# mLSTM output products by pairs of heads, sample transposes between the prompt chunks, and the sample state update beside the first attention scores

## What is computed

```python
s = jnp.einsum('blhd,bshd->bhls', q, k) * w_intra
num = (jnp.einsum('bhls,bshv->blhv', s, v)
       + jnp.einsum('bhvd,blhd->blhv', C, q) * jnp.moveaxis(w_inter, 1, 2)[..., None])
den = jnp.sum(s, axis=-1) + w_inter * jnp.einsum('bhd,blhd->bhl', n, q)
den = jnp.maximum(jnp.abs(den), jnp.exp(-m_t))
h = num / jnp.moveaxis(den, 1, 2)[..., None]
C_new = w_state[..., None, None] * C + jnp.einsum('bhs,bshv,bshd->bhvd', w_rows, v, k)
n_new = w_state[..., None] * n + jnp.einsum('bhs,bshd->bhd', w_rows, k)
```

## Time and profile before

| what | us |
|---|---|
| median of 3 runs | 1441.0 |
| lowest and highest of them | 1438.35 and 1442.01 |
| the profiled execution | 1432.52 |
| its span | 1430.7 |
| TensorE busy in the span | 1317.1 (92%) |
| from the first mLSTM score to the first attention score | 722.47 to 789.40 |

### The profile page before, as it was taken

The page is one execution under the profiler, slowest core; times in us unless marked ns, Lnnn a source line. Parts: engine busy times, 40 slices in busy tenths (PEclk is TensorE's granted clock), DMA queues, the critical chain, the costliest instruction groups (busy, mean ns, idle before and its releaser), DMA issues.

```text
span 1430.7 us, 23707 instructions
## 1 busy us (share of the span) xinstructions
PE 1317.1 (92%) x8072; PEld 1147.1 (80%) x8072; DVE 828.3 (58%) x1445; ACT 573.1 (40%) x1131; POOL 319.4 (22%) x276
## 2 busy tenths in 40 slices
PE   4999999999999969999997688969999999999996
PEld 2889999999778858888875355858899999988885
DVE  2666767776435455513335875338777777754545
ACT  4533434433334355322112465336444444433433
POOL 0443343433100000000100604004444444510000
PEclk9999999999999989999975698989999999999998
DMA  9545454544433322221220523112223322212232
GB/s 316 166 148 154 153 159 143 153 147 132 163 109 96 132 63 91 88 88 59 104 60 0 156 75 123 31 73 60 74 73 88 88 87 73 74 59 74 95 132 111
DMA packets 167003, 152.71 MB, mean 107 GB/s; under 512 B 10361, under 2 KB 139777, under 8 KB 166954
## 3 DMA queue, kind: packets, MB, share of 16 engines
q1 hardware_dynamic: 165610, 148.24, 33.0%
q0 software_dynamic: 1344, 3.81, 1.0%
HBM read 142.72 MB, written 9.05 MB: 106 GB/s over the span
## 4 chain that ended last, share of the span: by engine, by line
PE 79%; DVE 10%; issue 4%; ACT 4%; DMA 2%; DVEq 0%; POOL 0%; SPq 0%; ACTq 0%; POOLq 0%
PE ps L1079 76%; DVE resid L1942 1%; DVE w_sums_lo L1723 1%; DVE h_sums_lo L1723 1%; DVE max_den L2217 1%; DMA resid<-in_x_sample 1%; DMA w_raw<-in_w_ffn_in 1%; DVE act_t L1834 1%; DVE silu_gate L1827 1%; DVE w_lo L1723 1%; DVE probs L2226 1%; ACT x_norm L661 1%; PE ps L1121 0%; DVE y L1905 0%; ACT modulated_pairs L712 0%
## 5 line engine op out<-in xcount | busy, mean ns | idle before, releaser
L1079 PE MATMUL ps<-h_sums_hi,w_sums_hi 128*128 128x320 f32 x1216 | 378.0, 315 | 15.3 <-ACT silu_gate L731 5.0
L1079 PE MATMUL ps<-h_sums_hi,w_sums_lo 128*128 128x320 f32 x1216 | 370.7, 309 | 0.0
L1079 PE MATMUL ps<-h_sums_lo,w_sums_hi 128*128 128x320 f32 x1216 | 370.5, 309 | 0.0
L1079 PEld LDWEIGHTS ps<-h_sums_hi,w_sums_hi 128*128 128x128 f32 x1216 | 227.2, 188 | 31.9 <-issue 20.7
L1723 DVE TENSOR_TENSOR w_lo<-w_raw,w_hi 128x512 fp32r<-128x512 f32 (+3 forms) x106 | 99.0, 934 | 230.7 <-ACT w_hi L805 156.1
L1079 PEld LDWEIGHTS ps<-h_sums_lo,w_sums_hi 128*128 128x128 f32 x1216 | 227.2, 188 | 0.0
L1079 PEld LDWEIGHTS ps<-h_sums_hi,w_sums_lo 128*128 128x128 f32 x1216 | 227.1, 188 | 0.0
L1079 PE MATMUL ps<-w_hi,act_hi 128*128 128x512 f32 x440 | 174.0, 395 | 3.6 <-issue 3.6
L1079 PE MATMUL ps<-w_hi,act_lo 128*128 128x512 f32 x440 | 172.1, 391 | 0.0
L1079 PE MATMUL ps<-w_lo,act_hi 128*128 128x512 f32 x440 | 172.1, 391 | 0.0
L1723 DVE TENSOR_TENSOR w_sums_lo<-w_raw,w_sums_hi 128x512 fp32r<-128x512 f32 x136 | 129.1, 955 | 54.8 <-ACT w_sums_hi L749 45.0
(11 more groups left out here) (325 smaller groups left out, 1902.0 us busy)
## 6 DMA issues: line engine op xcount, KB each, us to landing
w_raw<-in_w_ffn_in SPq DMA_DIRECT2D x88, 512.0 KB, 3.8
w_raw<-in_w_ada SPq DMA_DIRECT2D x28, 1024.0 KB, 5.1
w_raw<-in_w_ffn_out SPq DMA_DIRECT2D x88, 256.0 KB, 2.6
w_raw<-in_w_in SPq DMA_DIRECT2D x10, 1024.0 KB, 5.1
w_raw_start<-in_w_ada SPq DMA_DIRECT2D x8, 1024.0 KB, 8.1
w_raw<-in_w_out SPq DMA_DIRECT2D x4, 1024.0 KB, 5.1
k_cache<-in_cache_k SPq DMA_DIRECT2D x8, 512.0 KB, 4.5
v_cache<-in_cache_v SPq DMA_DIRECT2D x8, 512.0 KB, 3.7
```

Of the source, the lines that this page charges most:

```text
L1079: return pe.matmul(out, lhsT, rhs, start=start, stop=stop)
```

## The change

Five things change.

1. PE's output products of a chunk go by pairs: `ST` for heads 0 and 1, then `QST` for heads 0 and 1, then the same for 2 and 3. DVE's `m_hn` waits become one wait for both banks.
2. The sample work is spread over the chunks. DVE writes `QB` for head 0 ahead of chunk 0 and for heads 1, 2 and 3 during chunks 0 and 1; PE transposes one set ahead of and one behind each chunk's output products (queries in chunks 0 and 1, states in chunks 2 and 3), all in bank 7; ACT copies each set between two exponentials. `QBT` has four buffers.
3. In the sample tile the `NROW` transpose and the `WB` products stand together in bank 7, and the 20 output products follow without transposes between them. DVE adds to `NNAT`, spreads the keys of heads 0 and 1 and scales `SC` while they run.
4. The prompt's final transposes and copy (to a tile of its own, `FIN`) come right behind these products, then the new states of heads 0 and 1, then the scores of attention steps 0 and 1, and then the new states of heads 2 and 3. DVE takes the first maxima and then adds all four new states and spreads the last two heads' keys.
5. The waits that stood ahead of the first score move to the first attention transposes and outputs. SP's `GH` loads wait for `st_tr` 5, and POOL's transfers out of `SC` for all of the new state.

```diff
-        QB = at("q_by_batch", N0, [P, DB, DQ]); N0 += 2 * KB
-        NROW = at("state_n_rows", N0 - 2 * KB, [32, P])
-        QBT = [at("q_by_batch_t0", N0, [P, DB // 2, P]), at("q_by_batch_t1", 20 * KB, [P, DB // 2, P])]; N0 += 2 * KB
+        QB = at("q_by_batch", N0, [P, DB, DQ])
...
+        QBT = [at(f"q_by_batch_t{h}", kb, [P, DB // 2, P]) for h, kb in enumerate((N0, 20 * KB, 26 * KB, 28 * KB))]; N0 += 2 * KB
+        FIN = at("state_c_prompt", N0, [P, 2, P]); N0 += KB
...
@@ -570,7 +569,7 @@
...
-                sp.wait_ge(n_mm, 1)
+                sp.wait_ge(st_tr, 5)
...
+            def transposed(n):
+                if n < HM:
+                    act.wait_ge(qb_tr, n + 1)
+                    act.activation(QBT[n][:, :, :], PS[:, 7, :].rearrange("p (r t) -> p r t", r=DB // 2), ACT.Copy).then_inc(qb_t, 1)
+                else:
+                    act.wait_ge(st_tr, n - HM + 1)
+                    act.activation(SCT[:, n - HM, :, 0:DV], PS[:, 7, :].rearrange("p (h v) -> p h v", h=HM), ACT.Copy).then_inc(st_t, 1)
             for c in range(NT):
                 act.wait_ge(m_arg, c + 1)
                 act.activation(ARG[c % 2][:, :, :], ARG[c % 2][:, :, :], ACT.Exp).then_inc(m_exp, 1)
...
+                if c:
+                    transposed(2 * c - 1)
+                if c < NTP:
+                    transposed(2 * c)
...
-            m_score(0)
...
+            def query_transposes(h):
+                pe.wait_ge(qb_ready, h + 1)
+                if h:
+                    pe.wait_ge(qb_t, h)
+                for r in range(DB // 2):
+                    q = pe.transpose(PS[:, 7, r * P:(r + 1) * P], QB[:, 2 * r:2 * r + 2, :], ident)
+                q.then_inc(qb_tr, 1)
+            def state_rows():
...
+                pe.transpose(PS[:, 7, 0:32], NROW[:, :], ident[0:32, 0:32])
...
+                for h in range(HM):
+                    q = mm(PS[0:DB, 7, (h + 1) * DQ:(h + 2) * DQ], WB[:, h, :], MK[:, NTP, h * DQ:(h + 1) * DQ])
+                q.then_inc(st_tr, 1)
+            def m_output(c):
                 pe.wait_ge(m_s, c + 1)
                 if c:
+                    pe.wait_ge(m_head, 2 * c)
+                if c == NTP:
+                    pe.wait_ge(st_n, 2)
+                    pe.wait_ge(qb_t, HM)
+                elif c:
                     pe.wait_ge(m_state, c)
-                    pe.wait_ge(m_head, 2 * c)
-                for h in range(HM):
-                    q = mm(m_out(c, h), ST[:, h, :], MVX[:, c, h, :], True, c == 0)
-                    if c:
-                        q = mm(m_out(c, h), QST[half(h), h // 2, c * P:(c + 1) * P], CTX[half(h), h // 2, :], False, True)
-                    if h >= 2:
-                        q.then_inc(m_hn, 1)
...
+                for pair in ((0, 1), (2, 3)):
...
+                    for h in pair:
+                        q = mm(m_out(c, h), ST[:, h, :], MVX[:, c, h, :], True, c == 0)
+                        if c == NTP:
+                            for r in range(DB // 2):
+                                q = mm(m_out(c, h), QBT[h][:, r, :], SCT[:, r, h, :], False, r == DB // 2 - 1)
+                    if c in range(1, NTP):
+                        for h in pair:
+                            q = mm(m_out(c, h), QST[half(h), h // 2, c * P:(c + 1) * P], CTX[half(h), h // 2, :], False, True)
+                            if h == 2:
+                                q.then_inc(m_hn, 1)
+                q.then_inc(m_hn, 1 if c in range(1, NTP) else 2)
+            m_score(0)
+            for c in range(NT):
+                if c < NTP:
+                    m_score(c + 1)
+                    m_state_part(c)
+                if c < 2:
+                    query_transposes(2 * c)
+                elif c < NTP:
+                    state_transposes(2 * c - 4)
+                else:
+                    state_rows()
+                m_output(c)
+                if c < 2:
+                    query_transposes(2 * c + 1)
+                elif c < NTP:
+                    state_transposes(2 * c - 3)
...
+            def state_update(h):
+                pe.wait_ge(kb_ready, h + 1)
+                if h == 1:
+                    pe.wait_ge(fin_c, 1)
+                else:
+                    pe.wait_ge(c_new, max(h, 1))
+                mm(PS[:, 7 - h % 2, :], MVX[:, NTP, h, 0:DV], KBM[h % 2][:, :, :]).then_inc(cu_s, 1)
             pe.wait_ge(m_state, NTP)
...
+            for j in range(2):
+                q = pe.transpose(PS[:, 6, j * P:(j + 1) * P], CTX[:, j, 0:DV], ident)
+            q.then_inc(fin_tr, 1)
+            state_update(0)
+            state_update(1)
...
             pe.wait_ge(m_s, NT)
-            pe.wait_ge(m_head, 2 * NTP)
-            for h in range(HM):
-                if h + 1 < HM:
-                    query_transposes(h + 1)
-                mm(m_out(NTP, h), ST[:, h, :], MVX[:, NTP, h, :], True, False)
-                pe.wait_ge(qb_t, h + 1)
-                for r in range(DB // 2):
-                    q = mm(m_out(NTP, h), QBT[h % 2][:, r, :], SCT[:, r, h, :], False, r == DB // 2 - 1)
-                q.then_inc(m_hn if h >= 2 else qb_mm, 1)
...
-            pe.wait_ge(fin_c, 1)
-            pe.wait_ge(m_s, NT)
-            pe.wait_ge(m_head, 2 * NT)
-            pe.wait_ge(c_new, HM)
-            pe.wait_ge(c_new, HM + 1)
...
@@ -1582,6 +1599,8 @@
             last_n = NTP * HD
             p_score(0)
             p_score(1)
+            state_update(2)
+            state_update(3)
             for n in range(last_n):
                 if n + 2 < last_n:
...
+            def queries_by_batch(h):
+                if h:
+                    dve.wait_ge(qb_tr, h)
+                dve.tensor_tensor(QB[:, :, :], MQG[:, NTP, h * DQ:(h + 1) * DQ].rearrange("p (b d) -> p b d", b=1).to_broadcast([P, DB, DQ]),
+                                  bmask.rearrange("p (b d) -> p b d", d=1).to_broadcast([P, DB, DQ]), ALU.mult).then_inc(qb_ready, 1)
...
+                if h == 0:
+                    dve.wait_ge(m_kw, NT)
+                    dve.wait_ge(qb_tr, HM)
...
+                    dve.wait_ge(m_s, NT)
+                else:
+                    dve.wait_ge(cu_s, h - 1)
+                dve.tensor_tensor(KBM[h % 2][:, :, :], KW[:, h, :].rearrange("p (b d) -> p b d", b=1).to_broadcast([P, DB, DQ]),
+                                  bmask.rearrange("p (b d) -> p b d", d=1).to_broadcast([P, DB, DQ]), ALU.mult).then_inc(kb_ready, 1)
+            def sample_state():
+                dve.wait_ge(st_tr, 5)
+                for a in range(2):
+                    r = slice(64 * a, 64 * a + 64)
+                    dve.tensor_copy(SCT[r, :, :, DV:DV + 1], PS[r, 7, 0:32].rearrange("p (r i h w) -> p i r h w", i=2, h=HM, w=1)[:, a, :, :, :]).then_inc(st_n, 1)
+                dve.tensor_tensor(NNAT[:, :, :], NNAT[:, :, :], PS[0:DB, 7, DQ:5 * DQ].rearrange("p (h d) -> p h d", h=HM), ALU.add).then_inc(c_new, 1)
+                keys_by_batch(0)
+                keys_by_batch(1)
+                link(dve.tensor_tensor(SC[:, :, :, :], SC[:, :, :, :],
+                                       WSB[:, 8:40].rearrange("p (h b d) -> p h b d", h=HM, d=1).to_broadcast([P, HM, DB, DQ]), ALU.mult))
             m_arguments(0)
             m_keys(0)
+            queries_by_batch(0)
             for c in range(NT):
                 dve.wait_ge(m_exp, c + 1)
...
+                    if c < 2:
+                        queries_by_batch(2 * c + 1)
                     dve.wait_ge(m_cu, c + 1)
...
-                    dve.wait_ge(st_tr, 5)
-                    for a in range(2):
-                        r = slice(64 * a, 64 * a + 64)
...
-                    for h in range(HM):
-                        if h:
-                            dve.wait_ge(qb_tr, h)
-                        dve.tensor_tensor(QB[:, :, :], MQG[:, c, h * DQ:(h + 1) * DQ].rearrange("p (b d) -> p b d", b=1).to_broadcast([P, DB, DQ]),
-                                          bmask.rearrange("p (b d) -> p b d", d=1).to_broadcast([P, DB, DQ]), ALU.mult).then_inc(qb_ready, 1)
+                    sample_state()
+                dve.wait_ge(m_hn, 2 * (c + 1))
...
                 for a in range(2):
-                    dve.wait_ge(m_hn, 2 * c + a + 1)
...
-            def keys_by_batch(h):
-                dve.wait_ge(m_s, NT)
-                dve.wait_ge(m_kw, NT)
-                if h >= 2:
...
+                if c == 0:
+                    queries_by_batch(2)
+                elif c == NTP - 2:
+                    dve.wait_ge(mst_landed, 16 * 7)
+                    link(dve.tensor_tensor(NNAT[:, :, :], NNAT[:, :, :], WS8[:, :].rearrange("p (h d) -> p h d", d=1).to_broadcast([DB, HM, DQ]), ALU.mult))
+            def new_state(h):
                 dve.wait_ge(cu_s, h + 1)
-                dve.tensor_tensor(SC[:, h, :, :], SC[:, h, :, :], PS[:, 6 + h % 2, :].rearrange("p (b d) -> p b d", b=DB), ALU.add).then_inc(c_new, 1)
-            dve.wait_ge(n_mm, 1)
```

(61 more changed lines are left out.)

48 lines of the change are left out of this document (8 added, 40 removed).

## The result

The changed kernel takes 1418.1 us in the median of 4 runs (1412.4 to 1419.67), beside 1439.7 for the kernel before (4 runs). The ratio is 0.9869, 95% interval 0.9843 to 0.9896: 18.9 us faster (15 to 23) where 9.9 were forecast. The profiled execution took 1412.4 us, the fastest of the four; its span is 1410.6.

A forecast was written before the change was run, and what follows sets the result against it. The prediction took PE to bound the kernel nearly everywhere, mostly at the low clock in this stretch. Its terms, +0.1 - 4.3 - 0.9 - 4.8 = -9.9 us, took the median from 1441.0 to 1431.1 us, range 1424 to 1440.5.

The forecast's parts named there:

- Step 1: Chunk loop: output products by pairs take 3.4 us per chunk, gaining 5.1 us together.
- rival C: Chunk loop: the `QST` pairs do not run together, so the gain is only 5.6 us, 1435.4; chance 0.06.
- Step 3: Bridge from the last chunk to the sample products: 3.8 us instead of 8.1, -4.3 us.
- step 2: Chunk loop: transposes moved in cost 5.15 us, so the loop ends where it ended, +0.1 us.
- Rival B: Chunks and sample products: dense work brings the high clock in more of the stretch, -16 us, 1425; chance 0.18.
- The likeliest case: Whole kernel: the forecast of -9.9 us, 1431.1, own range 1428 to 1435; chance 0.55.
- Steps 4 and 5: Sample products: 7.0 us against 7.9, -0.9; hand-over to attention's second maxima: 9.0 us against 13.8, -4.8.
- step 5: Hand-over: four additions and two `KBM` take 4.2 us at the high clock, 5.6 at the low, 5.1 assumed.
- rival D: Hand-over: the early scores do nothing and it stays at 13.8 us; -5.1 in all, 1436; chance 0.03.
- A: Chunks and sample products: the clock never rises there; only -1.7 us, 1439.3; chance 0.14.
- E: Sample attention: a low clock adds 2.4 us a step; six steps +14.4 us, 1445.6; all eight, 1450; chance 0.04.

The follow-up runs named there:

- run with filler transposes: The kernel before with eight transposes of `CON` by the identity added in each chunk, in the place of four filler products; 0.9945 of the kernel before.
- late-score trace: The changed kernel with all four new states and additions ahead of the first two attention scores; 0.9849 and 0.9852 of the kernel before.

## Why the prediction was wrong

**What held.** The kernel was bound where it said, and behind the stretch the two traces of the changed kernel are within 4.4 us of the two of the kernel before. Step 1 (pairs): two `QST` at once, 3.5 us a chunk measured against 3.4, in the run with pairs alone; rival C falls. Step 3 (bridge): -4.3 forecast and measured, with DVE's column copies last, as said; the same 3.7 to 3.8 in all traces of this order. That the additions on DVE's queue have no large gap held too (1.2 us at most, in the second trace).

**The term that failed** is the clock, in step 2's closing line, "what is open is the clock of these chunks", which the sum then took at the level of before: +0.1 us for the loop, measured -7.9 and, in the second trace, -10.9. Rival B had the mechanism, in the words that state products, transposes and two `ST` products now run densely in every chunk, and priced one chunk at the high clock, -16 us, 1425. In fact 72% of the stretch from the first score to the second maxima were at the high clock in the first trace and 64% in the second (means 0.86 and 0.82, against 0.63 before, where it was 26%), and the range ended at 1424. The likeliest case and rival B should have changed places: the trace of before had already shown the same sequence of state products and `ST` products ahead of the rise at 730, and that was put aside for the 40 us at the low clock behind it. These 40 us were no evidence on the new order, since they were spent in the head by head alternation, of which the change removes half the turns between heights.

**Steps 4 and 5.** The sample products were sized with the clock coming up 4.9 us after their start, 7.0 us. Measured 4.7 (all high) and 7.6 (low at first): the average, 6.2, is not far off, but the value depends on where the high clock falls. The hand-over was 7.6 and 8.6, forecast 9.0: in the first trace, all at the high clock, from the first addition to the second maxima it took 771.20 - 766.80 = 4.4 us, near the 4.2 that step 5 had for the high clock and not the 5.1 that it took. Its reason was partly wrong: the early scores brought nothing that could be measured, as the name of rival D says, but D's price, a hand-over that stays at 13.8, did not come; by elimination it was the work moved beneath the sample products that brought the gain.

**The other rivals.** A leaned on the 40 us at the low clock and on the rule that transposes do not bring it up. The chunks of the changed kernel, at 0.78 and 0.88, speak against the first, the times of the run with filler transposes against the second. E did not come: behind the second maxima the changed kernel took 639.4 and 643.0 us, the kernel before 639.6 and 638.6. One late-score trace and the trace with filler transposes had 646 us there. The 21.6 us of the first trace's stretch and 20.7 of the second agree with the 19 to 23 us of the times. POOL started 8.0 us behind the second maxima where 11.6 were forecast, since its transfers landed 3.7 us after the last issue and not 7.6; nothing measurable followed.

**What stays open.** Pairs alone lower the time at the low clock by 23 us over ten executions, but the one trace of them has a low clock in the chunks; where the high clock sat in the others is not known. How much of it needs the transposes beside them is therefore known from the times (12.4 us alone, 13 lost without them in the changed kernel) and not from traces. Which property of the order decides is open too: the number of turns between heights, the longer stretches of full-height work between them, or the two halves working at once. The runs change these together.

## What to carry to other kernels

When PE is busy all the time but at half its clock, as here, price the order of the work and not only its amount: sort products of the same height together, run half-height ones in pairs on opposite halves, and put waiting full-height work (transposes too) beside them. In this kernel the pairs were worth 12 to 13 us, of which only 5 are their own work. A cheap way to find out whether the clock is the bound is to add useless dense work at that place; if the kernel gets faster, it is. And an unknown clock is not a side remark of a forecast: give it its own two cases, worked out from rows at either level, before choosing the likeliest.

## What the runs showed of the hardware

Four float32 products a chunk with no use made the kernel 7.6 us faster (0.9947), the clock of the chunks going from 0.60 to 0.89 in the trace. Eight transposes a chunk did the same in the times (0.9945). Two half-height products on opposite halves took 0.73 us together at the low clock, as long as one alone. One kernel with the same instructions took 43.7 us at 0.59 in one execution and 33.7 at 0.81 in another. A change between full and half height costs about 0.3 us a product at the low clock (0.72 against 0.43).
